# Emptying a filler tile one step earlier, and starting the next projection before the last attention values, in a hybrid decoder layer

## The chip, the cores and the metric

The kernel runs on one core of a Trainium2 chip. The metric is the device time of one execution in microseconds. The core has a matrix engine (TensorE, PE in the rows; PEld is its loading of weights), VectorE (DVE), ScalarE (ACT), GpSimd (POOL) and SyncE (SP); each takes its own instructions strictly in order and waits on semaphores for the others. DMA transfers are issued by SP and POOL here.

## What is computed

One layer for 512 new tokens and 8 running sequences of 8 tokens each (576 columns in all). What matters here is the attention branch and what is multiplied after it:

```python
h = rmsnorm(x, p['norm1_w'])
proj = h @ p['w_in']
q, k, v, z, xbc, dt, ga, gb = jnp.split(proj, _split_points(IN_SIZES), axis=-1)
...
attn = stick_breaking_attention(q, k_all, v_all, sb_bias, past)
...
merged = jax.nn.sigmoid(ga) * (attn @ p['w_pa']) + jax.nn.sigmoid(gb) * (y @ p['w_pb'])
x = x + merged @ p['w_out']
```

In stick-breaking attention a weight is the sigmoid of its logit times the product of (1 - sigmoid) over later keys, a running product along the keys. All products are taken in three parts (high x high, low x high, high x low) to hold float32 accuracy. After this come the SSD mixer, the output projection and the feed-forward part.

## The kernel before, in words

**A tile** is one 128 x 576 result of a dense product, kept in one of two buffers of PSUM, `G[0]` and `G[1]` (`tile_banks`), by the parity of its number. `product` (L437 to L453) multiplies one slice of 128 inputs into it with six matmuls; a tile has 8 slices (`KD`). It waits before the first slice until the buffer is free (`tile_free`), which the engine that reads the tile signals. A weight chunk of 128 columns is loaded by SP, copied to `w_hi` by ScalarE (`make_hi`, L417) and its rest to `w_lo` by VectorE (`make_lo`, L423); chunks alternate between two buffers.

**Attention** is a software pipeline of 60 steps (`STEPS_A`) over 57 units: one for new keys, 16 for cache pages, 40 for the prompt (8 pairs of heads, five units each). In step t TensorE makes the logits of unit t (L1120), ScalarE their sigmoid (L1679) and one minus it (L1692), VectorE the running product and the weights one step later (`weigh`, L2177 and L2179), TensorE turns the weights of unit t-2 (L1145), ScalarE copies them out (`read_weights`, L1715) and VectorE takes the rest (L2223). In the step three after a pair's last unit TensorE multiplies values with weights, 16 matmuls (`weigh_values`, L1200), whose result lies in `G[0]`; ScalarE (L1748) and VectorE (L2242) read it, and ScalarE (L1753) and VectorE (L2248) split it into the two parts that the projection will multiply.

**Fillers** are 22 tiles (both gates and six tiles of z) whose slices are laid between this work: `filler_steps` gives each step up to two slices in its middle (after the logits) and up to two (for the prompt one) at its end. They all use `G[1]`, since `G[0]` holds turned keys and the values' result; so filler f has tile number `T_FILL + 2 * f`. When a tile is finished one place is left empty, then the next tile begins. 17 of the 22 end in the middle of their step: 3 while pages are read, and 14 in the prompt's steps 17, 20, 23 and so on to 56; three end at the end of a page step, filler 21 at the end of step 57, and filler 0 before the steps.

`gate_tile(f)` on ScalarE waits until the tile is done, copies it out through the sigmoid (L1723), which frees the buffer, and then makes the `w_hi` of chunk f+2. It stands at the head of the step after the one in which the tile ended. VectorE makes that chunk's `w_lo` in that next step, and GpSimd stores the tile (`store_gate`, L806).

**The drain** is steps 57 to 59, without logits. Step 59 has the last values product. Behind it TensorE waits until VectorE has read `G[0]` (`pv_read`, 16) and makes the eight tiles of `attn @ w_pa` (L1233 to L1239); the first uses `G[0]`. The result of each is multiplied by VectorE (L2281) with a gate tile that GpSimd brings back from memory (`ga_in`, L811). Before GpSimd asks for it, it does in its order: store filler 21, make `a_seq` (L823), clear a scratch array with six DMAs (L826), wait for them, set a diagonal (L828).

Of the kernel before, what the change touches and what calls it, by code (L numbers as in the profile page):

```python
# [123 lines left out]
def build(nc, x_prompt, x_sample, cache_k, cache_v, page_table, state_ssm, state_conv, norm1_w, w_in,  # L124
# [21 lines left out]

    T_FILL = N_FIRST
    assert T_FILL % 2 == 1
    T_PA = T_FILL + 2 * N_FILL - 1
    T_SSD = T_PA + KD  # L150
    T_OUT = T_SSD + NG * (10 + KD) - len(Z_EARLY)
    T_FFN = T_OUT + KD
# [2 lines left out]
    with ExitStack() as ctx:  # L155
# [5 lines left out]
        def sem(name):  # L161
            if name not in sems:
                sems[name] = ctx.enter_context(nc.semaphore(name))
            return sems[name]
# [275 lines left out]
        def product(pe, t, w, x, start=True, stop=True, rows=P, step=0, i=0, onto=False):  # L440


            if start:
                pe.wait_ge(tile_free[t % 2], half(t, step, i) + 1)
            last = len(w) - 1
            for k, ((wh, wl), (xh, xl)) in enumerate(zip(w, x)):
                for h in range(2):
                    out = G[t % 2][0:rows, h, 0:HALF]
                    nc.tensor.matmul(out, wh, xh[:, HALVES[h]], start=start and k == 0, stop=False, skip_group_check=onto)  # L449
                    nc.tensor.matmul(out, wh, xl[:, HALVES[h]], start=False, stop=False, skip_group_check=onto)  # L450
                for h in range(2):
                    out = G[t % 2][0:rows, h, 0:HALF]
                    mm = nc.tensor.matmul(out, wl, xh[:, HALVES[h]], start=False, stop=stop and k == last, skip_group_check=onto)  # L453
            return mm
# [112 lines left out]
                    tile_end[f] = (n - 1) // 2  # L567
        late_tiles = [f for f in range(N_FILL) if f not in tile_end]
        ends_at = {t: [f for f in tile_end if tile_end[f] == t] for t in range(-1, STEPS_A)}

        def filler_tile(f):
            return T_FILL + 2 * f
# [50 lines left out]
        def out_hi(k):  # L623
            return qo[:, 2 * k, :]
# [364 lines left out]
        def _(pe):  # L989
# [50 lines left out]
            def fill(todo):  # L1040


                for f, k in todo:
                    c, t = C_FILL + f, filler_tile(f)
                    if k == 0:
                        pe.wait_ge(split, c + 1)
                    mm = product(pe, t, [(w_hi[:, c % 2, k, :], w_lo[:, c % 2, k, :])], [(x_hi[:, k, :], x_lo[:, k, :])], start=k == 0, stop=k == KD - 1)
                    if k == KD - 1:
                        mm.then_inc(tile_done, 2 if f else 1)
# [154 lines left out]
            def turn_outputs(part):  # L1204
# [5 lines left out]
                    mm = pe.transpose(out_bank(part)[:, b * P:(b + 1) * P], o_rows[:, b * P:(b + 1) * P], ident[:, :])  # L1210
                mm.then_inc(sem("o_turned"), 1)

            for t in range(STEPS_A):
                if t < NU:
                    logits(units[t])
                if is_page(t + 1):
                    turn_keys(t + 1)
                for part in range(2):
                    if t == 2 * SEQS * (part + 1) + 6:
                        turn_outputs(part)  # L1220
                fill(filler[1 + 2 * t])
                if t >= 3:
                    weigh_values(units[t - 3])
                if 2 <= t < NU + 2:
                    if t == 2 * SEQS + 6:
                        pe.wait_ge(sem("o_lo_made"), 1)
                    turn_weights(units[t - 2])
                fill(filler[2 + 2 * t])
            fill(filler[-1])

            pe.wait_ge(sem("pv_read"), 2 * KD)
            pe.sem_inc(tile_free[0], N_FILL - 1)
            for n in range(KD):  # L1233
                c, t = C_PA + n, T_PA + n
                pe.wait_ge(split, c + 1)
                for k in range(KD):
                    if n == 0:
                        pe.wait_ge(sem("o_split"), k + 1)
                    mm = product(pe, t, [(w_hi[:, c % 2, k, :], w_lo[:, c % 2, k, :])], [(out_hi(k), out_lo(k))], start=k == 0, stop=k == KD - 1)  # L1239
                mm.then_inc(tile_done, 1)  # L1240


# [290 lines left out]
        def _(act):  # L1533
# [220 lines left out]

            for t in range(STEPS_A + 2):
                for f in ends_at.get(t - 1, []):
                    gate_tile(f)
                if t < NU:
                    stick(units[t])
                if is_page(t + 1):  # L1760
                    read_keys(t + 1)
                if t < NU:
                    stick_rest(units[t])
                for part in range(2):
                    if t == 2 * SEQS * (part + 1) + 6:
                        outputs_hi(part)
                if 2 <= t < NU + 2:
                    read_weights(units[t - 2])
                for part in range(2):
                    if t == 2 * SEQS * (part + 1) + 3:  # L1770
                        copy_outputs(part)
                if 4 <= t < NU + 4 and units[t - 4]["kind"] == "prompt" and units[t - 4]["last"]:
                    pair_hi(units[t - 4]["p"])
                if 3 <= t < NU + 3 and units[t - 3]["kind"] == "prompt" and units[t - 3]["last"]:
                    lower_half(units[t - 3]["p"])
# [853 lines left out]
```

## Time and profile before

| | us |
|---|---|
| median of 3 runs | 1492.87 |
| lowest, highest | 1485.05, 1494.22 |
| the profiled execution's own time | 1489.72 |
| its span, first to last instruction | 1488.2 |
| TensorE matmul busy | 1417.5 (95%) |
| VectorE busy | 822.6 (55%) |
| ScalarE busy | 654.4 (44%) |
| GpSimd busy | 222.4 (15%) |
| TensorE idle before the first matmul of a slice of `x_hi`, whole span | 18.0, of it 14.0 released by ScalarE's L1723 |

The chain of waits of the page is empty here (its last piece is a DMA that was issued at the end), so the profile is read by waits and by timelines. The steps of attention run from about 140 to 428 us, the `attn @ w_pa` tiles follow until 484 us; the SSD mixer, the output projection and the feed-forward products come behind them.

### The profile page before, as it was taken

Reading aid. Unit: us, or ns where it says so; the run is one execution under the profiler, and the core shown is the slowest. Engines: PE = TensorE matmul, PEld = TensorE weight load, DVE = VectorE, ACT = ScalarE, POOL = GpSimd, SP = SyncE. Lnnn points to the kernel's source line nnn. Section 1 sums busy time; section 2 is a strip of 40 time slices with the busy share of each in tenths; the row PEclk is TensorE's granted clock in tenths of the full one; section 3 lists DMA queues with packets and bytes.
Section 4 is the critical chain, followed back from the end, with each engine's and each line's share of the span. In section 5 each row is a group of like instructions: output and inputs, shape, how many; then the busy total and the mean of one; then the engine's idle time right before and its main releaser. Section 6 shows DMA issues by size and latency. Waiting matters only on the chain. (4 is left out here: it accounts for less than half of the span.)

```text
span 1488.2 us, 27180 instructions
## 1 busy us (share of the span) xinstructions
PE 1417.5 (95%) x10645; PEld 1332.1 (90%) x10645; DVE 822.6 (55%) x1194; ACT 654.4 (44%) x1086; POOL 222.4 (15%) x398
## 2 busy tenths in 40 slices
PE   4999999989989999999999999999999999999997
PEld 4998777888879988889988988899999999999997
DVE  3554545887742566777687675774444444442221
ACT  4565454766631354574364473434432333331221
POOL 3002232000021213322222213211100000000000
PEclk9999999999999999999999999999999999999999
DMA  3225674221256433434334425352223222223331
GB/s 116 72 78 169 177 213 146 67 61 59 67 126 195 97 92 109 113 103 114 101 114 109 114 72 177 109 191 71 86 71 88 81 85 85 85 81 100 95 93 48
DMA packets 201109, 157.35 MB, mean 106 GB/s; under 512 B 13672, under 2 KB 187216, under 8 KB 200959
## 3 DMA queue, kind: packets, MB, share of 16 engines
q1 hardware_dynamic: 175394, 97.93, 23.0%
q0 software_dynamic: 25232, 57.70, 13.5%
q8 instruction: 66, 1.08, 0.3%
q10 hardware_dynamic: 384, 0.37, 0.1%
q14 instruction: 33, 0.27, 0.1%
HBM read 132.04 MB, written 23.91 MB: 105 GB/s over the span
## 5 line engine op out<-in xcount | busy, mean ns | idle before, releaser
L449 PE MATMUL tile_banks<-x_hi,w_hi 128*128 128x288 f32 (+1 forms) x1808 | 530.9, 308 | 18.0 <-ACT gate_out L1723 14.0
L450 PE MATMUL tile_banks<-x_lo,w_hi 128*128 128x288 f32 (+1 forms) x1808 | 508.3, 296 | 0.0
L453 PE MATMUL tile_banks<-x_hi,w_lo 128*128 128x288 f32 (+1 forms) x1808 | 386.9, 295 | 0.0
L449 PEld LDWEIGHTS tile_banks<-x_hi,w_hi 128*128 128x128 f32 (+1 forms) x1808 | 341.9, 189 | 33.5 <-issue 25.3
L450 PEld LDWEIGHTS tile_banks<-x_lo,w_hi 128*128 128x128 f32 (+1 forms) x1808 | 342.1, 189 | 4.7 <-issue 3.6
L423 DVE TENSOR_TENSOR w_lo<-w_raw,w_hi 128x1024 fp32r<-128x1024 f32 (+2 forms) x169 | 208.3, 1233 | 174.7 <-ACT w_hi L417 173.5
L453 PEld LDWEIGHTS tile_banks<-x_hi,w_lo 128*128 128x128 f32 (+1 forms) x1808 | 291.4, 188 | 0.4
L417 ACT ACTIVATE w_hi<-w_raw 128x1024 fp32r<-128x1024 f32 (+2 forms) x169 | 175.7, 1039 | 103.6 <-PE tile_banks L453 102.0
L450 PE MATMUL tile_banks<-f_lo,w_hi 128*128 128x288 f32 x352 | 98.3, 295 | 0.0
L449 PE MATMUL tile_banks<-f_hi,w_hi 128*128 128x288 f32 x352 | 97.8, 294 | 0.0
L453 PE MATMUL tile_banks<-f_hi,w_lo 128*128 128x288 f32 x352 | 73.9, 291 | 0.0
L980 POOL DMA_DIRECT2D out_y_prompt<-y_tok x8 | 6.2, 779 | 410.1 <-ACT y_tok L2050 410.1
L2037 ACT ACTIVATE f_hi<-prod 128x576 f32 (+1 forms) x22 | 15.1, 686 | 118.3 <-DVE prod L2575 118.3
L450 PEld LDWEIGHTS tile_banks<-f_lo,w_hi 128*128 128x128 f32 x352 | 66.2, 188 | 0.0
L449 PEld LDWEIGHTS tile_banks<-f_hi,w_hi 128*128 128x128 f32 x352 | 66.0, 188 | 0.0
L2306 DVE SCALAR_TENSOR_TENSOR conv_acc<-conv_src,conv_par,conv_acc 128x600 f32<-128x600 f32 x72 | 60.8, 844 | 2.5
L1837 ACT ACTIVATE conv_src<-tile_banks 128x288 f32<-128x288 f32 x24 | 9.9, 412 | 118.6 <-PE tile_banks L453 118.6
L787 POOL DMA_DIRECT2D v_page<-in_cache_v x64 | 34.5, 539 | 160.0 <-issue 160.0
L449 PE MATMUL tile_banks<-y_hi,w_hi 128*128 128x288 f32 x192 | 56.8, 311 | 0.2 <-DVE w_lo L423 0.2
L453 PEld LDWEIGHTS tile_banks<-f_hi,w_lo 128*128 128x128 f32 x352 | 56.5, 188 | 0.0
L450 PE MATMUL tile_banks<-y_lo,w_hi 128*128 128x288 f32 x192 | 53.7, 295 | 0.0
L2177 DVE TENSOR_TENSOR_SCAN after_w<-rest,zero_col 128x128 f32<-128x128 f32 (+2 forms) x64 | 52.4, 818 | 0.3
(378 smaller groups left out, 2501.2 us busy)
## 6 DMA issues: line engine op xcount, KB each, us to landing
w_raw<-in_w_in SPq DMA_DIRECT2D x68, 512.0 KB, 3.8
w_raw<-in_w_gate SPq DMA_DIRECT2D x22, 512.0 KB, 3.8
w_raw<-in_w_up SPq DMA_DIRECT2D x22, 512.0 KB, 3.7
k_page<-in_cache_k SPq DMA_DIRECT2D x64, 128.0 KB, 2.6
v_page<-in_cache_v POOLq DMA_DIRECT2D x64, 128.0 KB, 3.0
old<-in_state_ssm POOLq DMA_DIRECT2D x32, 256.0 KB, 3.4
out_ssm_sample<-old POOLq DMA_DIRECT2D x32, 256.0 KB, 2.8
w_raw<-in_w_pb SPq DMA_DIRECT2D x16, 512.0 KB, 3.6
```

Of the source, the lines that this page charges most:

```text
L417: nc.scalar.activation(w_hi[:, c % 2, 0:tiles, 0:width], w_raw[:, c % 2, 0:tiles, 0:width], ACT.Copy).then_inc(hi_made, 1)
L423: nc.vector.tensor_tensor(w_lo[:, c % 2, 0:tiles, 0:width], w_raw[:, c % 2, 0:tiles, 0:width], f32(w_hi[:, c % 2, 0:tiles, 0:width]), ALU. ...
L449: nc.tensor.matmul(out, wh, xh[:, HALVES[h]], start=start and k == 0, stop=False, skip_group_check=onto)
L450: nc.tensor.matmul(out, wh, xl[:, HALVES[h]], start=False, stop=False, skip_group_check=onto)
L453: mm = nc.tensor.matmul(out, wl, xh[:, HALVES[h]], start=False, stop=stop and k == last, skip_group_check=onto)
L787: eng.dma_start(v_page[:, n % V_SLOTS, :], cache_v[0, bass.ds(page_of(eng, x, k), 1)].rearrange("o p h d -> p (o h d)")).then_inc(sem(f"v_ ...
L980: eng.dma_start(y_prompt[0].rearrange("(c p) n -> p c n", p=P)[:, :, bass.ds(P * i, P)], y_tok[:, 0:NC, :]).then_inc(sem("y_out"), 16)
L1837: eng.activation(dst[:, 3:3 + HALF], G[t % 2][:, 0, 0:HALF], ACT.Copy)
L2037: eng.activation(f_hi[:, bass.ds(2 * i + n, 1), :], prod2[:, n:n + 1, :], ACT.Copy).then_inc(sem("f_hi_made"), 1)
L2177: link(eng.tensor_tensor_scan(out=after_w[:, slot, edge - width:edge][:, ::-1], data0=rest[:, slot, cols][:, ::-1], data1=zero_col[:, 0:1] ...
L2306: ins = eng.scalar_tensor_tensor(out=dst, in0=src[:, w:w + m], scalar=conv_par[:, w * CT + ct:w * CT + ct + 1], in1=dst, op0=ALU.mult, op1 ...
```

## The change

ScalarE empties a tile that ended in the middle of its step in that same step: after its sigmoid work, before it copies out the turned weights. `ends_mid` lists these tiles; the 5 others stay as they were. VectorE's and GpSimd's orders are unchanged. `T_PA` grows by one, so that the first `w_pa` tile lies in `G[1]` and not in `G[0]`; all later tiles swap buffers with it. Its first four slices are issued at the end of step 58, the next three in step 59 ahead of the last values product, the eighth behind it. The wait for `pv_read` now stands behind that tile.

```diff
--- before.py
+++ after.py
@@ -146,7 +146,7 @@
 
     T_FILL = N_FIRST
     assert T_FILL % 2 == 1
-    T_PA = T_FILL + 2 * N_FILL - 1
+    T_PA = T_FILL + 2 * N_FILL
     T_SSD = T_PA + KD
     T_OUT = T_SSD + NG * (10 + KD) - len(Z_EARLY)
     T_FFN = T_OUT + KD
@@ -567,6 +567,8 @@
                     tile_end[f] = (n - 1) // 2
         late_tiles = [f for f in range(N_FILL) if f not in tile_end]
         ends_at = {t: [f for f in tile_end if tile_end[f] == t] for t in range(-1, STEPS_A)}
+        ends_mid = {t: [f for f, k in filler[1 + 2 * t] if k == KD - 1] for t in range(STEPS_A)}
+        assert not late_tiles and not filler[2 * STEPS_A - 2] and not filler[2 * STEPS_A - 1]
 
         def filler_tile(f):
             return T_FILL + 2 * f
@@ -1210,6 +1212,15 @@
                     mm = pe.transpose(out_bank(part)[:, b * P:(b + 1) * P], o_rows[:, b * P:(b + 1) * P], ident[:, :])
                 mm.then_inc(sem("o_turned"), 1)
 
+            def first_pa(slices):
+
+                c = C_PA
+                pe.wait_ge(split, c + 1)
+                for k in slices:
+                    pe.wait_ge(sem("o_split"), k + 1)
+                    mm = product(pe, T_PA, [(w_hi[:, c % 2, k, :], w_lo[:, c % 2, k, :])], [(out_hi(k), out_lo(k))], start=k == 0, stop=k == KD - 1)
+                return mm
+
             for t in range(STEPS_A):
                 if t < NU:
                     logits(units[t])
@@ -1219,6 +1230,8 @@
                     if t == 2 * SEQS * (part + 1) + 6:
                         turn_outputs(part)
                 fill(filler[1 + 2 * t])
+                if t == STEPS_A - 1:
+                    first_pa(range(PG, KD - 1))
                 if t >= 3:
                     weigh_values(units[t - 3])
                 if 2 <= t < NU + 2:
@@ -1226,17 +1239,16 @@
                         pe.wait_ge(sem("o_lo_made"), 1)
                     turn_weights(units[t - 2])
                 fill(filler[2 + 2 * t])
-            fill(filler[-1])
+                if t == STEPS_A - 2:
+                    first_pa(range(PG))
+            first_pa(range(KD - 1, KD)).then_inc(tile_done, 2)
 
             pe.wait_ge(sem("pv_read"), 2 * KD)
-            pe.sem_inc(tile_free[0], N_FILL - 1)
-            for n in range(KD):
+            pe.sem_inc(tile_free[0], N_FILL)
+            for n in range(1, KD):
                 c, t = C_PA + n, T_PA + n
                 pe.wait_ge(split, c + 1)
-                for k in range(KD):
-                    if n == 0:
-                        pe.wait_ge(sem("o_split"), k + 1)
-                    mm = product(pe, t, [(w_hi[:, c % 2, k, :], w_lo[:, c % 2, k, :])], [(out_hi(k), out_lo(k))], start=k == 0, stop=k == KD - 1)
+                mm = product(pe, t, [(w_hi[:, c % 2, k, :], w_lo[:, c % 2, k, :]) for k in range(KD)], [(out_hi(k), out_lo(k)) for k in range(KD)])
                 mm.then_inc(tile_done, 1)
 
 
@@ -1754,7 +1766,8 @@
 
             for t in range(STEPS_A + 2):
                 for f in ends_at.get(t - 1, []):
-                    gate_tile(f)
+                    if f not in ends_mid.get(t - 1, []):
+                        gate_tile(f)
                 if t < NU:
                     stick(units[t])
                 if is_page(t + 1):
@@ -1764,6 +1777,8 @@
                 for part in range(2):
                     if t == 2 * SEQS * (part + 1) + 6:
                         outputs_hi(part)
+                for f in ends_mid.get(t, []):
+                    gate_tile(f)
                 if 2 <= t < NU + 2:
                     read_weights(units[t - 2])
                 for part in range(2):
```

The place is ScalarE's order in step 29, in which filler 11 ends and a values product lies as well. `wt_hi` is the copy of turned weights, `o_part` the reading of the values' result, `gate_out` the tile and `w_hi` the chunk behind it. Before:

```order
L1679 ACTIVATE beta<-spare_bank,bias_all 128x256 x2
L1692 ACTIVATE rest<-beta 128x512
L1715 ACTIVATE wt_hi<-spare_bank 128x4x128
L1748 ACTIVATE o_part<-tile_banks 64x512 x2
L1723 ACTIVATE gate_out<-tile_banks 128x576
L417 ACTIVATE w_hi<-w_raw 128x1024
```

With the change:

```order
L1691 ACTIVATE beta<-spare_bank,bias_all 128x256 x2
L1704 ACTIVATE rest<-beta 128x512
L1735 ACTIVATE gate_out<-tile_banks 128x576
L417 ACTIVATE w_hi<-w_raw 128x1024
L1727 ACTIVATE wt_hi<-spare_bank 128x4x128
L1760 ACTIVATE o_part<-tile_banks 64x512 x2
```

The tile and the chunk's `w_hi` have moved ahead of `wt_hi` and `o_part`; the four other rows kept their order.

The second place is TensorE's order in the drain, at the last turning of weights (`<-ident,beta`) in step 58. Before, the last values product (`wt_hi,v_hl`) follows it directly:

```order
L453 MATMUL tile_banks<-x_hi,w_lo 128x288 x2
L1145 MATMUL spare_bank<-ident,beta 128x128 x4
L1200 MATMUL tile_banks<-wt_hi,v_hl 128x512
L1200 MATMUL tile_banks<-wt_lo,v_hl 128x512
L1200 MATMUL tile_banks<-wt_hi,v_hl 128x384
```

With the change products of the projection (`qo`) follow it:

```order
L453 MATMUL tile_banks<-x_hi,w_lo 128x288 x2
L1147 MATMUL spare_bank<-ident,beta 128x128 x4
L449 MATMUL tile_banks<-qo,w_hi 128x288
L450 MATMUL tile_banks<-qo,w_hi 128x288
L449 MATMUL tile_banks<-qo,w_hi 128x288
```

Seven slices stand there, 35 such rows, and then the values product begins:

```order
L450 MATMUL tile_banks<-qo,w_hi 128x288
L453 MATMUL tile_banks<-qo,w_lo 128x288 x2
L1202 MATMUL tile_banks<-wt_hi,v_hl 128x512
L1202 MATMUL tile_banks<-wt_lo,v_hl 128x512
L1202 MATMUL tile_banks<-wt_hi,v_hl 128x384
```

The eighth slice comes behind that product:

```order
L1202 MATMUL tile_banks<-wt_hi,v_hl 128x128
L1202 MATMUL tile_banks<-wt_lo,v_hl 128x128
L449 MATMUL tile_banks<-qo,w_hi 128x288
L450 MATMUL tile_banks<-qo,w_hi 128x288
L449 MATMUL tile_banks<-qo,w_hi 128x288
```

The values product has thus moved behind seven of the eight slices of the first tile.

## Rows read from the trace of the kernel before

**Rows 1.** Waits of TensorE, 125 to 490 us: us in total, times, longest.

```profile
PE tile_banks L449 <- ACT gate_out L1723: 14.0, 14, 2.0
```

**Rows 2.** Timeline of TensorE: start, us, operation; in brackets idle before it and releaser.

```profile
303.42 0.37 PE L449 MATMUL tile_banks<-x_hi,w_hi 128*128 128x288 f32 x1 [1.97 <-ACT gate_out L1723]
...
313.82 0.37 PE L449 MATMUL tile_banks<-x_hi,w_hi 128*128 128x288 f32 x1 [0.60 <-ACT gate_out L1723]
...
327.59 0.37 PE L449 MATMUL tile_banks<-x_hi,w_hi 128*128 128x288 f32 x1 [1.29 <-ACT gate_out L1723]
...
338.21 0.37 PE L449 MATMUL tile_banks<-x_hi,w_hi 128*128 128x288 f32 x1 [0.66 <-ACT gate_out L1723]
...
351.27 0.37 PE L449 MATMUL tile_banks<-x_hi,w_hi 128*128 128x288 f32 x1 [0.78 <-ACT gate_out L1723]
...
415.39 0.37 PE L449 MATMUL tile_banks<-x_hi,w_hi 128*128 128x288 f32 x1 [1.32 <-ACT gate_out L1723]
```

**Rows 3.** Timeline of ScalarE in step 29.

```profile
300.77 0.60 ACT L1715 ACTIVATE wt_hi<-spare_bank 128x512 fp32r<-128x512 f32 x1 [3.11 <-PE spare_bank L1145]
301.39 1.21 ACT L1748 ACTIVATE o_part<-tile_banks 64x512 f32<-64x512 f32 x2
302.62 0.65 ACT L1723 ACTIVATE gate_out<-tile_banks 128x576 f32<-128x576 f32 x1
303.17 1.05 ACT L417 ACTIVATE w_hi<-w_raw 128x1024 fp32r<-128x1024 f32 x1
```

**Rows 4.** Windows: length, busy time of each engine, granted clock, DMA share.

```profile
300.00:375.00 75.00, 67.73 (x488) 63.03 (x488) 59.83 (x92) 50.49 (x87) 3.25 (x6) 0.98 0.22 66
```

**Rows 5.** Timeline of VectorE, steps 30 and 31, up to the end of unit 30's weights.

```profile
306.35 0.69 DVE L2223 TENSOR_TENSOR wt_lo<-spare_bank,wt_hi 128x512 fp32r<-128x512 f32 x1 [0.62 <-ACT wt_hi L1715]
...
310.60 0.29 DVE L2179 TENSOR_TENSOR beta<-beta,after_w 128x128 f32<-128x128 f32 x1
```

**Rows 6.** Timeline of TensorE, step 32, turning of unit 30's weights.

```profile
311.90 0.60 PE L1145 MATMUL spare_bank<-ident,beta 128*128 128x128 f32 x4
```

**Rows 7.** Timeline of ScalarE in step 38.

```profile
336.93 0.60 ACT L1715 ACTIVATE wt_hi<-spare_bank 128x512 fp32r<-128x512 f32 x1 [0.59 <-PE spare_bank L1145]
```

**Rows 8.** Timeline of VectorE in step 38.

```profile
337.56 0.69 DVE L2223 TENSOR_TENSOR wt_lo<-spare_bank,wt_hi 128x512 fp32r<-128x512 f32 x1 [0.87 <-ACT wt_hi L1715]
```

**Rows 9.** Timeline of TensorE, values product of step 39.

```profile
339.85 0.39 PE L1200 MATMUL tile_banks<-wt_hi,v_hl 128*128 128x512 f32 x1
```

**Rows 10.** Windows of 2 us in which the clock fell during attention.

```profile
366.00:368.00 2.00, 2.00 (x11) 2.00 (x12) 1.90 (x5) 1.97 (x4) 0.54 (x1) 0.67 0.38 147
368.00:370.00 2.00, 2.00 (x11) 1.99 (x11) 0.27 (x1) 0.67 (x3) 0.00 (x0) 0.50 0.00 0
```

**Rows 11.** Timeline of TensorE in the drain and the first projection tiles.

```profile
425.31 0.50 PE L1200 MATMUL tile_banks<-wt_hi,v_hl 128*128 128x512 f32 x1 [2.46 <-DVE wt_lo L2223]
...
430.50 0.37 PE L449 MATMUL tile_banks<-qo,w_hi 128*128 128x288 f32 x1 [2.43 <-PEq L1232]
...
438.47 0.29 PE L449 MATMUL tile_banks<-qo,w_hi 128*128 128x288 f32 x1
...
445.19 0.40 PE L449 MATMUL tile_banks<-qo,w_hi 128*128 128x288 f32 x1 [0.31 <-DVE w_lo L423]
```

**Rows 12.** Timeline of ScalarE in the drain, filler 21.

```profile
422.45 0.65 ACT L1723 ACTIVATE gate_out<-tile_banks 128x576 f32<-128x576 f32 x1 [2.62 <-PE tile_banks L453]
```

**Rows 13.** Timeline of VectorE in the drain.

```profile
430.90 0.69 DVE L2248 TENSOR_TENSOR qo<-o_sum,qo 128x512 fp32r<-128x512 f32 x1 [0.70 <-ACT qo L1753]
...
443.24 0.76 DVE L2281 TENSOR_TENSOR gate_out<-tile_banks,ga_in 128x576 f32<-128x576 f32 x1 [11.65 <-DMA ga_in<-gates_dram]
```

**Rows 14.** Timeline of GpSimd in the drain.

```profile
439.55 0.56 POOL L828 DMA_DIRECT2D sums_dram<-ones  x1 [9.52 <-DMA sums_dram<-zeros]
```

**Rows 15.** Windows of 2 us after two pauses of TensorE.

```profile
432.00:434.00 2.00, 2.00 (x10) 2.00 (x10) 0.00 (x0) 0.00 (x0) 0.00 (x0) 0.50 1.49 223
...
488.00:490.00 2.00, 2.00 (x8) 1.78 (x8) 0.00 (x0) 0.66 (x4) 0.81 (x2) 0.50 0.46 62
```

## The prediction, made before the changed kernel was run

> **What bounds the kernel now.** I first read the waits of TensorE over attention and the tiles behind it [rows 1]: 14.0 us in 14 waits are one kind, the first slice of a filler tile held back until ScalarE has emptied the tile before it. The timeline [rows 2] shows these waits one by one. There are 14 because 14 fillers end in the middle of a prompt step; they come in six sizes: 0.60 (3 times), 0.66 (3), 0.78 (3), 1.29 (2), 1.97 (2) and 1.32 (once), together 13.96. The reader should see that each stands on TensorE itself, which has no other work in order at that point. Then the windows [rows 4]: in 75 us of attention TensorE is busy 67.7, VectorE 59.8, ScalarE 50.5. TensorE sets the pace, but VectorE is 80% busy, so a delay given to VectorE may come back. Last I read the drain [rows 11 to 14], engine by engine.
>
> **Part one: the tile is emptied in its own step.** ScalarE does the same work; the 0.65 for the tile and 1.05 for the next chunk's `w_hi` [rows 3] only change places with the copy of the turned weights. In step 29 the order was: wait 3.11 for the turned weights behind the values product, 0.60, then `o_part` 1.21, then the tile. Now tile and `w_hi` fit into those 3.11 and TensorE's wait of 1.97 goes. In a step without a values product, as step 38 [rows 7], ScalarE was idle 0.59 from 336.34 to 336.93, waiting for the turning that TensorE does behind the tile. The tile can be emptied from about 336.5 to 337.15, and TensorE wants the buffer at 338.21 - 0.66 = 337.55 [rows 2]: this wait goes too.
>
> What the move costs: `wt_hi` comes later, and VectorE's `wt_lo` behind it. In step 38: tile to 337.15, `w_hi` to 338.1, `wt_hi` to 338.6 and not 337.53, so `wt_lo` starts at 338.65 and not 337.56 [rows 8] and ends at 339.33. TensorE's values product needs it, and would now start at 339.85 - 0.66 = 339.19 [rows 9]. So 0.15 of the 0.66 is given back. If the 1.29 of step 35 has just been gained, VectorE is behind by about 0.3 more and 0.45 of 1.29 + 0.66 is given back: 1.5 is kept.
>
> The other place is behind the 1.97. VectorE finished the weights of unit 30 at 310.60 + 0.29 = 310.89 and TensorE turned them at 311.90 [rows 5, 6], a margin of 1.0. TensorE would be there 1.97 earlier, at 309.93; VectorE gains only the 0.62 that it had waited for `wt_hi` [rows 5], and ends at 310.3. TensorE waits 0.4 there. ScalarE's (1 - sigmoid) of a new unit needs the same weights to be finished, so it gets to filler 12 late and 0.2 more is left there: of 1.97 + 0.60 I keep 2.0. In the next values product VectorE waits anyway, so nothing is carried on from pair to pair.
>
> The 0.78 waits I count as gone. For the 1.32 in front of filler 21 no logits lie between, so TensorE wants the buffer right after the turning: 0.6 is left. The sum: 2 x 2.0 (1.97 with 0.60) + 2 x 1.5 (1.29 with 0.66) + 3 x 0.78 + 0.60 + 0.5 (the 0.60 and the 0.66 that stand alone) + 0.7 (the 1.32) = 11.1 us. Its bounds: 14.0 if VectorE is never late, and about 1 if the 1.1 us by which `wt_hi` moved in step 38 returned at the 12 tiles that end without a values product (14.0 - 13.2). I take 11.1, near the top, because the rows show a margin at most of these places. The three fillers that end mid-step under the pages had no wait before; their ScalarE move is hidden by its waits for turned weights. I count nothing.
>
> With the 1.97 goes something else. Behind the second of the two, at 365.96, the granted clock was 0.67 and then 0.50 for 2 us each [rows 10]: 1.2 GHz and not 2.4. Work lost: 0.66 + 1.00 = 1.66 us. Behind the first of them it did not fall. I take it that without the pause the clock stays up: 1.6 us. Bounds 0 and 1.6.
>
> **Part two: seven slices before the last values product.** Before, TensorE had two pauses [rows 11]: 2.46 until 425.31 and 2.43 until 430.50. Tile 1 begins at 438.47 and ends at 445.19 - 0.31 = 444.88, 6.41 for 8 slices, 0.80 each. With the change, in times of before: ScalarE frees filler 21's buffer at 422.45 + 0.65 = 423.10 [rows 12], TensorE starts at 423.25, and seven slices last to 428.85. The values product (425.31 to 430.50 - 2.43 = 428.07, 2.76) runs to 431.6. The eighth slice needs the last pair's low part; VectorE ended it at 430.90 + 0.69 = 431.59, 3.52 behind the values product [rows 13], so now at 435.1. That is a new pause of 3.5 in place of 4.9 in two. Tile 0 ends at 435.9, 2.6 earlier than 438.47, and tile 1 at 442.3.
>
> But tile 2 needs a `w_lo` which stands on VectorE behind the multiplication of tile 0 with its gate, and this started at 443.24 only because the gate's transfer landed then; VectorE had waited 11.65 for it [rows 13]. The transfer hangs on GpSimd, which waited 9.52 for its clearing DMAs until 439.55 [rows 14]; these follow the store of filler 21, not TensorE's projection. Their time moves with filler 21, by part one, and not by part two. So tile 2 starts at 445.19 less part one's gain, as before. **Part two is worth no more than 0.3**, the 0.31 that tile 2 waited for its `w_lo`; the 2.6 turn into a pause of 2.9 in front of tile 2. Bounds: 2.6 if the transfer came sooner, -1.7 by the clock (below). Changing the buffers' parity adds no instruction and I count it at nothing: the buffer of every later tile is read by the same engine in the same order.
>
> **The sum** on the profiled execution's own 1489.7: 1489.7 - 11.1 - 1.6 - 0.3 = 1476.7. That execution was 3.2 below the median of the three runs (1492.9), whose spread is 9; the forecast for a median is thus about 3 higher: **1480**.
>
> **The rivals.**
>
> *A. The clock falls once more in front of tile 2.* TensorE would pause 3.5 before slice eight and 2.9 before tile 2. Pauses of 2.43 and 2.20 were each followed by a clock of 0.50 [rows 15]. A fall behind the first pause is hidden, it shortens the second; one behind the second is not: 1.7 us as in attention [rows 10]. That gives 1481.7. Against it: if the first pause lowers the clock, tile 1 ends near 444 and the second pause is only about 1.3. The Trainium skill (TensorE: Matmul & The Clock Gate, section on HAM oscillation) says that waits between bursts of matmuls send the clock back to half rate so that the next burst starts slow; it speaks against part two, and by it the sum would be about 1.7 higher. Chance 0.2.
>
> *B. VectorE takes the gain back.* The moved `wt_hi` makes `wt_lo` and the next weights late at most tiles, or ScalarE reaches the tile late, so that the change does not empty it earlier. For it: VectorE is 80% busy [rows 4], and margins of 0.2 to 1.0 us are what I worked with. Against it: it waits in every values product. Between 1 and 7 us remain in all: 1486 to 1492 for a median, middle 1489. Chance 0.17.
>
> *C. Everything goes.* No wait is left (14.0), the clock stays up (1.6), and the transfer comes early enough for 2.6 in the drain: 18.2, 1474.7 for a median. Chance 0.14.
>
> *D. Slower: VectorE becomes the bound.* If VectorE had no slack, each of the 17 mid-step tiles would push `wt_hi` and all behind it by 0.65 + 1.05 = 1.7: 28.9 lost, 14.0 recovered, 1508. It decides once the pushes exceed VectorE's idle time. In 75 us that is 15.2 [rows 4], against 5 tiles with 8.5. So it should not: chance 0.04.
>
> **The numbers.** The forecast has 0.45, A 0.2, B 0.17, C 0.14, D 0.04. The range that leaves out the far parts of B, C and D is 1472 to 1489: it holds part one between 8 and 14, the clock either way, about 3 us between one median and the next, and the nearer half of B. One per cent is 14.9 us, about what a measurement of this kernel can tell from no change. C and the upper half of the forecast's spread lie beyond it: faster 0.30, same 0.66, slower 0.04.
>
> **What would show it.** In the waits of TensorE the line on ScalarE's tile copy falls from 14.0 to between 0.5 and 2, and new waits of some tenths on VectorE's weights (L1145 before) and `wt_lo` appear, 1 to 3 us in all. VectorE's wait for the gate's transfer stays near 8 us (its own last work, at 435.1, is 3.5 later than before, and the transfer lands at the same distance behind filler 21), and TensorE shows a pause of about 3.5 behind the last values product and one of 2 to 3 on `w_lo` in front of tile 2. From there on the two traces run at a constant distance of 11 to 13 us. I am wrong if filler 21 ends less than 8 us earlier than before, if tile 2 starts at another distance behind filler 21 than 22.7, or if the distance changes in the later stages.

## The result and the profile after

The changed kernel takes 1482.8 us (median of 9 runs, 1480.2 to 1485.1) against 1494.0 of the kernel before (9 runs, 1485.1 to 1496.2): a ratio of 0.9931 with a 95% interval of 0.9915 to 0.9948. That is 10.3 us by the ratio and 11.2 between the two medians, within the 1% at which the forecast called it the same, and inside its range of 1472 to 1489. The profiled execution took 1482.8 us with a span of 1481.3; the one of before, 1489.7 and 1488.2, lay 4.3 below that kernel's median.

The waits of TensorE in the changed kernel, 125 to 490 us (total, times, longest). The first row is a pause that the kernel before did not have; the third answers [rows 1]:

```profile
PE tile_banks L449 <- DVE qo L2263: 3.7, 1, 3.7
...
PE tile_banks L1202 <- DVE wt_lo L2238: 1.4, 3, 0.8
...
PE tile_banks L449 <- ACT gate_out L1735: 0.8, 2, 0.4
...
PE spare_bank L1147 <- DVE beta L2194: 0.8, 2, 0.4
...
PE tile_banks L449 <- DVE w_lo L423: 0.4, 1, 0.4
```

The waits on ScalarE's tile copy fell from 14.0 us to 0.8, and one of the two that are left (0.40) is the new one in front of the projection's first slice. Added to them are 0.8 on VectorE's weights (L2194) and 1.4 on `wt_lo`: 3.0 in all, so 11.0 of 13.96 are gone. The prediction had 11.1. Three of the places, in the timeline of TensorE:

```profile
275.85 0.50 PE L1202 MATMUL tile_banks<-wt_hi,v_hl 128*128 128x512 f32 x1 [0.84 <-DVE wt_lo L2238]
...
308.39 0.65 PE L1147 MATMUL spare_bank<-ident,beta 128*128 128x128 f32 x4 [0.39 <-DVE beta L2194]
...
402.77 0.37 PE L449 MATMUL tile_banks<-x_hi,w_hi 128*128 128x288 f32 x1 [0.41 <-ACT gate_out L1735]
```

The first is the values product behind the 0.66 that stood alone; it gives back 0.84, where about 0.15 was worked out. The second is the turning of unit 30's weights [rows 6], which now waits 0.39 (0.4 was worked out). The third stands where 1.32 stood in front of filler 21 [rows 2], with 0.41 left (0.6 was worked out).

The drain, as TensorE, ScalarE, VectorE and GpSimd have it; these answer [rows 11 to 14]:

```profile
422.54 0.58 PE L449 MATMUL tile_banks<-qo,w_hi 128*128 128x288 f32 x1 [3.67 <-DVE qo L2263]
...
432.61 0.40 PE L449 MATMUL tile_banks<-qo,w_hi 128*128 128x288 f32 x1 [0.44 <-DVE w_lo L423]
```

```profile
409.78 0.65 ACT L1735 ACTIVATE gate_out<-tile_banks 128x576 f32<-128x576 f32 x1 [2.53 <-PE tile_banks L453]
```

```profile
421.70 0.69 DVE L2263 TENSOR_TENSOR qo<-o_sum,qo 128x512 fp32r<-128x512 f32 x1 [0.69 <-ACT qo L1765]
...
430.67 0.76 DVE L2296 TENSOR_TENSOR gate_out<-tile_banks,ga_in 128x576 f32<-128x576 f32 x1 [8.28 <-DMA ga_in<-gates_dram]
```

```profile
426.96 0.56 POOL L830 DMA_DIRECT2D sums_dram<-ones  x1 [9.59 <-DMA sums_dram<-zeros]
```

Filler 21 is emptied 12.67 us earlier than before (409.78 for 422.45), and tile 2 of the projection starts 12.58 earlier (432.61 for 445.19), so 22.83 behind filler 21 where it was 22.74. The early start of tile 0 brought nothing to that point: VectorE waited 8.28 for the gate's transfer, and GpSimd 9.59 for its clearing DMAs (9.52 before).

But the pause in front of tile 2 is 0.44 and not the 2.9 of the forecast. The windows of 2 us around slice eight show why (length, busy time and instructions of PE, PEld, DVE, ACT, POOL, then the granted clock, DMA share, GB/s):

```profile
418.00:420.00 2.00, 0.87 (x7) 0.72 (x5) 0.40 (x1) 1.07 (x2) 0.00 (x0) 1.00 1.38 259
420.00:422.00 2.00, 0.00 (x0) 0.00 (x0) 1.27 (x3) 0.74 (x2) 0.00 (x0) 0.68 1.34 185
422.00:424.00 2.00, 1.47 (x6) 1.50 (x7) 0.39 (x1) 0.00 (x0) 0.00 (x0) 0.50 1.33 162
424.00:426.00 2.00, 2.00 (x10) 2.00 (x9) 0.00 (x0) 1.06 (x1) 0.00 (x0) 0.50 0.68 88
426.00:428.00 2.00, 2.00 (x11) 2.00 (x11) 0.00 (x0) 0.00 (x0) 1.04 (x2) 0.61 0.02 3
428.00:430.00 2.00, 2.00 (x17) 2.00 (x16) 0.00 (x0) 0.00 (x0) 0.68 (x2) 1.00 0.68 201
```

The clock falls inside the pause of 3.67 and stays at 0.50, which is 1.2 GHz, until past 427: fully busy, TensorE starts 10 matmuls in the window at 424 and 17 in the one at 428. Tile 1 ends 22.4 behind filler 21, and 19.9 had been worked out at full clock. How much of it is lost differs from execution to execution: in a second profile of the same kernel the half clock lasted half as long, tile 1 ended 21.7 behind filler 21, and the pause in front of tile 2 was longer:

```profile
432.72 0.40 PE L449 MATMUL tile_banks<-qo,w_hi 128*128 128x288 f32 x1 [1.42 <-DVE w_lo L423]
```

### The profile page after: what moved, and what is told of

It reads as the page before. It is cut to its first block and busy times, and to the rows that moved or that the text cites. A ratio compares the mean times of both kernels' runs of the same rounds, so it can differ in the third digit from the quotient of the medians.

```text
span 1481.3 us, 27182 instructions
## 1 busy us (share of the span) xinstructions
PE 1422.3 (96%) x10645; PEld 1336.3 (90%) x10645; DVE 823.6 (56%) x1194; ACT 653.2 (44%) x1086; POOL 221.4 (15%) x398
```

## The stages side by side

The starts of VectorE's `w_lo` instructions cut the execution into stages. "Attention" is from filler 2's `w_lo` to filler 21's copy on ScalarE, "projection" from there to the `w_lo` of the first SSD chunk, "SSD" from it to the last SSD chunk's, "middle" to the 16th gate/up chunk's, "dense" to the last chunk's. All are differences of starts in the timelines, in us. "Falls" counts periods at half clock between 500 and 990 us, taken from windows of 10 us (one period takes 1.7 off the sum of clock times length).

| kernel (one profile each) | attention | projection | SSD | falls | middle | dense | span |
|---|---|---|---|---|---|---|---|
| before | 278.65 | 55.81 | 511.07 | 2 | 160.81 | 317.75 | 1488.2 |
| before again | 278.69 | 55.98 | 507.14 | 0 | 160.61 | 321.77 | 1490.9 |
| changed | 266.12 | 55.91 | 512.76 | 3 | 160.37 | 322.15 | 1481.3 |
| changed again | 266.30 | 56.22 | 508.64 | 0 | 161.20 | 322.88 | 1478.9 |
| part one alone | 265.99 | 56.66 | 508.43 | 1 | 163.18 | 321.85 | 1479.6 |
| part two alone | 280.47 | 55.75 | 511.17 | 2 | 161.87 | 322.88 | 1495.2 |
| eight slices behind | 266.56 | 55.68 | 512.31 | 3 | 162.89 | 318.65 | 1479.9 |
| 4 + 4, late transfer | 266.23 | 56.82 | 512.31 | 3 | 164.01 | 322.84 | 1487.2 |
| early transfer | 266.67 | 55.37 | 513.37 | 4 | 162.82 | 318.84 | 1482.0 |
| part one, early transfer | 266.32 | 56.84 | 511.19 | 2 | 162.67 | 318.64 | 1479.3 |
| `w_hi` later | 265.52 | 55.78 | 507.59 | 0 | 160.00 | 322.58 | 1473.4 |
| 4 + 4, early transfer | 266.70 | 50.49 | 511.38 | 3 | 160.82 | 322.89 | 1476.7 |
| the two together | 265.86 | 50.51 | 508.17 | 1 | 162.54 | 322.57 | 1473.3 |
| two tiles only | 274.45 | 56.66 | 509.65 | 2 | 160.61 | 321.26 | 1486.2 |

The columns "attention" and "projection" hold the effects of the edits. SSD, falls, middle and dense show no pattern that follows the edits, and the span adds everything up, which is why the whole times of single profiles mislead. The middle stage took 162.5 or more in the six profiles that have a period at half clock in it, and 160.0 to 161.9 in the others.

## Experiments

Every timed kernel ran beside the kernel before on the same chip.

**Part one alone.** The kernel before with `ends_mid` on ScalarE:

```diff
                 for f in ends_at.get(t - 1, []):
-                    gate_tile(f)
+                    if f not in ends_mid.get(t - 1, []):
+                        gate_tile(f)
...
+                for f in ends_mid.get(t, []):
+                    gate_tile(f)
                 if 2 <= t < NU + 2:
                     read_weights(units[t - 2])
```

Expected: 

> Only ScalarE's early emptying; the projection's first tile stays behind the values product and in G[0]. Theory 1 (part one is the whole gain): the waits on ScalarE's tile copy fall from 14.0 to about 1, filler 21 ends 12 to 13 us earlier than before (at about 410), tile 2 of the projection starts 22.7 behind filler 21's emptying, and the ratio to before is that of the full change, 0.993. Rival (part two carries 2 us or more of the gain): ratio 0.9945 or higher, and tile 2 starts 25 behind filler 21.

Measured: 1480.3 us, ratio 0.9906 (0.9882 to 0.9930). Attention is 265.99 long, as in the full change, and filler 21 is emptied at 409.11. The projection is 0.4 to 0.75 longer than in the two profiles of the changed kernel: tile 2 starts 23.71 behind filler 21, between the 22.7 of theory 1 and the 25 of the rival, and without a wait, since here TensorE itself is late (the clock fell behind both pauses of the drain). So part one is the gain.

**Part two alone.** The changed kernel with `gate_tile` back at the head of the next step:

```diff
                 for f in ends_at.get(t - 1, []):
-                    if f not in ends_mid.get(t - 1, []):
-                        gate_tile(f)
+                    gate_tile(f)
...
-                for f in ends_mid.get(t, []):
-                    gate_tile(f)
```

Expected: 

> Only the early start of the projection's first tile and its buffer; ScalarE empties every tile in the next step as before. Theory 1: the 14 waits stay at 14.0 us, tile 0 is done 2 to 3 us earlier, but tile 2 starts at the same distance behind filler 21 (22.7), so ratio 1.000. Rival (part two gains): 0.998 or lower. Second rival (the new pause lowers the clock): 1.001.

Measured: ratio 1.0004 (0.9986 to 1.0021), the projection 55.75: nothing, as expected. The 14 waits on ScalarE's tile copy in attention came to 14.0 us again; two more outside it make 16 and 14.8. Its attention is 1.8 longer than before's: TensorE waited 1.25 longer for key pages (3.21 against 1.96), and was busy 0.56 longer, with 6.83 us at half clock against 4.40. Here the clock falls behind both waits of 1.97, at 304 and at 368, and not behind the second alone [rows 10]:

```profile
304.00:306.00 2.00, 2.00 (x12) 1.98 (x10) 0.90 (x2) 0.79 (x2) 0.00 (x0) 0.50 0.34 126
...
368.00:370.00 2.00, 2.00 (x11) 1.98 (x10) 1.02 (x2) 1.07 (x4) 0.00 (x0) 0.50 0.38 147
```

**All eight slices behind the values product**, in the buffer and with the parities of the change:

```diff
-                if t == STEPS_A - 1:
-                    first_pa(range(PG, KD - 1))
...
-                if t == STEPS_A - 2:
-                    first_pa(range(PG))
-            first_pa(range(KD - 1, KD)).then_inc(tile_done, 2)
+            first_pa(range(KD)).then_inc(tile_done, 2)
```

Expected: 

> The full change, but all eight slices of the first tile stand behind the last values product; its buffer is still G[1] and all later tiles keep the swapped buffers. Theory 1: time as the full change and as part one alone, 0.993, since tile 2 waits for the gate's transfer in all of them. Rival (swapping the buffers' parity is what slows the gate and up products, seen as 0.81 us a slice after and 0.78 before): the feed-forward stretch is slower here and in the part-two kernel, and fast in the part-one kernel.

Measured: ratio 0.9943 (0.9922 to 0.9965), projection 55.68. Tile 2 starts 22.61 behind filler 21, once more on its `w_lo`:

```profile
432.66 0.40 PE L449 MATMUL tile_banks<-qo,w_hi 128*128 128x288 f32 x1 [2.74 <-DVE w_lo L423]
```

Tile 1 thus ends 19.88 behind filler 21, 2.5 sooner than in the changed kernel's first profile and in the kernel before. With the other buffer the first slice need not wait for `pv_read`, and that alone gives what part two was to give, without the pause of 3.67. The seven early slices are worth nothing. The rival on the buffers' parity fell: this kernel's dense stage is fast (318.65) and part one's, with the old parities, slow (321.85).

**The changed kernel again**, unaltered.

Expected: 

> The changed kernel unaltered, for one more profile. Theory: the slower pace of the feed-forward slices (0.81 and not 0.78) comes and goes from execution to execution; then the profiles of the four kernels of this call differ in it without regard to their buffers. Rival: it belongs to the swapped buffers and is here again.

Measured: ratio 0.9934 (0.9909 to 0.9959), dense stage 322.88, slow again. That alone would fit the rival; the kernel above decides against it, and so does the kernel before in its second profile (below).

**The gate's transfer earlier.** GpSimd asks for the first two gate tiles right behind the store of filler 21:

```diff
             for f in ends_at[STEPS_A - 1] + late_tiles:
                 store_gate(f)
+            for n in range(2):
+                gate_back(n)
...
-            for n in range(2):
-                gate_back(n)
```

Expected: 

> The full change, and GpSimd asks for the first two gate tiles right behind the store of filler 21, before it clears its scratch array. Theory 1 (the transfer's lateness ate part two): VectorE no longer waits for it, tile 2 starts when tile 1 ends, 20 us behind filler 21's emptying and not 22.8, and the time falls by 2.5 to 3 us against the full change: 0.991 of before. Rival (something else holds tile 2, as the chunk's w_hi or the clock behind the 3.7 us pause): tile 2 at 22 or more and 0.993.

Measured: ratio 0.9902 (0.9864 to 0.9939), and the projection 55.37, only 0.5 to 0.9 shorter than the changed kernel's two and not 2.5 to 3. VectorE no longer waits for the transfer, so half of theory 1 holds, but tile 2 comes hardly sooner, 22.42 behind filler 21 where the theory had 20 and the rival 22 or more. The ratio is near the theory's 0.991, but its interval holds the rival's 0.993 too. The rival's second guess is what holds tile 2: the clock, in windows of 4 us:

```profile
420.00:424.00 4.00, 0.44 (x5) 0.29 (x3) 2.06 (x3) 1.81 (x3) 0.00 (x0) 0.82 1.32 179
424.00:428.00 4.00, 3.90 (x16) 3.93 (x17) 1.69 (x2) 1.06 (x1) 0.00 (x0) 0.50 1.19 147
428.00:432.00 4.00, 4.00 (x28) 4.00 (x27) 0.29 (x1) 0.00 (x0) 1.57 (x3) 0.83 0.66 160
```

Tile 0's last slice and nearly half of tile 1 (3.7 of its 8.0 us) run at 1.2 GHz behind the pause of 3.66. Two limits of nearly the same length stood one behind the other, and taking one away shows the other.

**Part one alone with the earlier transfer** (the same edit on the part-one kernel).

Expected: 

> Part one alone with the same earlier transfer, the projection's first tile behind the values product. Theory 1: before, tile 2 waited only 0.3 beyond tile 1, so the earlier transfer brings 0.3 here, ratio 0.993; with the kernel above this makes part two worth 2.5 us once the transfer is early. Rival (part two worth nothing even then): both 0.991 or both 0.993.

Measured: ratio 0.9907 (0.9874 to 0.9940), projection 56.84 against 56.66: nothing. By the projection, part two with the early transfer is thus worth 56.84 - 55.37 = 1.5 us, not the 2.5 expected; the two ratios, 0.9902 and 0.9907, are as the rival had them, and their intervals are too wide to show 1.5 us. In both part-one kernels the clock fell twice in the drain, behind each of the two pauses of 2.4 to 2.5, and tile 1 ended later than in the kernel before, where it fell once.

**Slices four and four around the values product, transfer early:**

```diff
-                if t == STEPS_A - 1:
-                    first_pa(range(PG, KD - 1))
...
-            first_pa(range(KD - 1, KD)).then_inc(tile_done, 2)
+            first_pa(range(PG, KD)).then_inc(tile_done, 2)
```

Expected: 

> The full change with the earlier transfer, and the first tile's slices laid four before and four behind the last values product. Theory 1: the last pair's low part is ready 2.4 us earlier, three slices run while it is made, the pause of 3.7 falls to about 1.3, and with no long pause the clock need not fall: 2 to 4 us less than with the earlier transfer alone, 0.989 of before. Rival (the end of the gates' chain on VectorE is already the bound): no more than 0.991.

Measured: 1477.1 us, ratio 0.9884 (0.9848 to 0.9921), projection 50.49: 4.9 us shorter than with the earlier transfer alone and 5.4 shorter than the change. The pause fell to 1.18 and the clock stayed up:

```profile
418.00:422.00 4.00, 2.82 (x22) 2.59 (x21) 2.06 (x3) 1.34 (x3) 1.38 (x2) 1.00 1.34 226
422.00:426.00 4.00, 4.00 (x32) 4.00 (x32) 1.98 (x2) 1.06 (x1) 0.00 (x0) 1.00 1.25 163
426.00:430.00 4.00, 4.00 (x33) 4.00 (x32) 1.12 (x2) 1.06 (x1) 0.00 (x0) 1.00 0.87 173
```

VectorE in the same kernel; the third gate tile is the next to be late, 7.82 of waiting that TensorE does not yet feel:

```profile
422.16 0.76 DVE L2294 TENSOR_TENSOR gate_out<-tile_banks,ga_in 128x576 f32<-128x576 f32 x1 [1.15 <-PE tile_banks L453]
...
438.68 0.76 DVE L2294 TENSOR_TENSOR gate_out<-tile_banks,ga_in 128x576 f32<-128x576 f32 x1 [7.82 <-DMA ga_in<-gates_dram]
```

**Four and four, transfer late** (the same edit on the changed kernel).

Expected: 

> The full change with the slices laid four and four, but the gate's transfer as late as before. Theory 1 (transfer is the limit in the drain): the pause of 3.7 is gone and the clock stays up, tile 1 ends 18 to 19 behind filler 21's emptying, but tile 2 still starts at 22.7 and TensorE waits about 4 there; time as the full change, 0.993. Rival (the clock was the limit): tile 2 starts at 20 or less and 0.990.

Measured: ratio 0.9930 (0.9913 to 0.9948), projection 56.82, 6.3 longer than with the early transfer. The timeline of TensorE and its windows:

```profile
421.13 0.40 PE L449 MATMUL tile_banks<-qo,w_hi 128*128 128x288 f32 x1 [1.18 <-DVE qo L2261]
...
433.25 0.61 PE L449 MATMUL tile_banks<-qo,w_hi 128*128 128x288 f32 x1 [4.83 <-DVE w_lo L423]
```

```profile
431.00:433.00 2.00, 0.00 (x0) 0.00 (x0) 1.69 (x2) 0.00 (x0) 0.64 (x2) 0.98 0.09 37
433.00:435.00 2.00, 1.75 (x7) 1.75 (x8) 1.99 (x3) 0.00 (x0) 1.28 (x3) 0.50 0.62 196
435.00:437.00 2.00, 2.00 (x13) 2.00 (x12) 0.00 (x0) 0.00 (x0) 0.23 (x1) 0.67 0.81 232
```

Tile 2 starts at 433.25, 22.38 behind filler 21, as the theory had it, behind a pause of 4.83 in which TensorE had nothing to do. Tile 1 ended 17.55 behind filler 21 and the clock had stayed up until then. But at the end of this pause it falls, and tile 2 takes 7.80 where it took 6.45 in the changed kernel: that is rival A of the prediction, here in its pure form, at 1.35 and not 1.7. Neither edit gives anything alone (0.5 and -0.9); together they give 5.4.

**`w_hi` stays in the next step,** only the tile's copy moves:

```diff
                 for f in ends_at.get(t - 1, []):
                     if f not in ends_mid.get(t - 1, []):
                         gate_tile(f)
+                    else:
+                        make_hi(C_FILL + f + 2, after_tiles=filler_tile(f) + 1)
...
                 for f in ends_mid.get(t, []):
-                    gate_tile(f)
+                    gate_tile(f, hi=False)
```

Expected: 

> The full change, but of the two ScalarE instructions only the tile's emptying moves into its own step; the next chunk's w_hi stays at the head of the next step. Theory 1 (what is left of the gain is lost to the turned weights' copy, pushed by 1.7 us): the push is now 0.65, the waits on VectorE's weights and wt_lo (0.8 and 1.4 us) shrink to under 1 in all, and 1 us more is gained: 0.992. Rival (the loss is VectorE's own load, not the push): these waits stay at 2 us and 0.993.

Measured: ratio 0.9920 (0.9889 to 0.9951), attention 265.52, 0.6 to 0.8 shorter than in the changed kernel. The waits left:

```profile
PE spare_bank L1147 <- DVE beta L2197: 1.1, 3, 0.5
...
PE tile_banks L449 <- ACT gate_out L1735: 1.1, 3, 0.5
...
PE tile_banks L1202 <- DVE wt_lo L2241: 0.7, 1, 0.7
```

They come to 2.9, where the changed kernel's two profiles have 3.0 and 3.3. The waits on `wt_lo` halved, those on the weights rose. Some of the shorter stage is the wait for key pages, 2.3 us here against 2.4 and 3.3. The ratio is the 0.992 of theory 1, but the waits on the weights and `wt_lo`, which it put at under 1, come to 1.8. So theory 1 is not borne out: at most a few tenths hang on the push of `wt_hi`, and most of what is left does not.

**Both together** (`w_hi` later, four and four, transfer early).

Expected: 

> The transfer early, slices four and four around the last values product, and the chunk's w_hi left in the next step. Theory 1: the pieces add up: attention 0.5 to 0.8 us shorter, then 20 to 21 us from filler 21's emptying to the start of tile 2's successor as with the split alone; 1474 to 1477 by the level of the feed-forward pace, 0.987 to 0.989 of before.

Measured: 1476.7 us, ratio 0.9888 (0.9866 to 0.9910). Attention 265.86 and projection 50.51 add up. This version and the four-and-four split with the early transfer are the fastest here, and the intervals do not tell the two apart. That split, 0.9884 (0.9848 to 0.9921), lies below the changed kernel's 0.9931 (0.9915 to 0.9948), but the intervals just overlap; what shows its gain is the projection.

**Two tiles only.** Part one for fillers 11 and 16, those with waits of 1.97:

```diff
-        ends_mid = {t: [f for f, k in filler[1 + 2 * t] if k == KD - 1] for t in range(STEPS_A)}
+        ends_mid = {t: [f for f, k in filler[1 + 2 * t] if k == KD - 1 and t in (29, 44)] for t in range(STEPS_A)}
```

Expected: 

> Before, with the early emptying for two of the 17 tiles only, fillers 11 and 16, whose waits were 1.97 each. Theory 1: the waits on ScalarE's tile copy fall from 14.0 to about 10, the clock does not fall at 366 us nor at 303, and attention (from the w_lo at 143 us to filler 21's emptying) is shorter than before's 278.65 by 3.9 + 1.66 less the 0.4 that VectorE's weights cost twice: 273.5 to 274.5. Rival (the clock's falls there have nothing to do with the 1.97 waits): a fall is still seen and 275 or more.

Measured (one run, 1487.7 us): attention 274.45, inside the 273.5 to 274.5. The wait and its count:

```profile
PE tile_banks L449 <- ACT gate_out L1724: 10.5, 13, 1.3
```

No window of 2 us between 142 and 424 us has a lowered clock. The books of attention: 3.93 less waiting on the tiles (13.95 to 10.02; the 13th wait, 0.44, lies ahead of the stage), 0.77 more on VectorE's weights, 1.56 more on key pages (3.52 against 1.96), so TensorE was idle 1.60 less. It also spent 4.4 us fewer at half clock, 3.4 of them at 366 and 1.0 at the stage's start, which is worth 2.2. That makes 3.8, and the stage became 4.2 shorter. The remaining 0.4 I can't name, and the longer key-page waits and the 1.0 at the start were not foreseen, so the number falls into the expected interval partly by chance; the absence of the falls does not depend on it.

**The kernel before again.**

Expected: 

> The kernel before, unaltered, for one more profile. Theory: 14.0 us of waits again, the clock falls behind neither, one or both of the 1.97 waits, and its feed-forward slices run at 0.78 or at 0.81 us, the pace being no property of the kernel.

Measured (one run, 1492.4 us): 14.0 us in 14 waits, attention 278.69, the clock fell once behind such a wait, at 369, and the dense stage took 321.77 where the first profile of the same kernel took 317.75.

## Why the prediction held, point by point

**Waits on the tile's copy:** right in kind and in the total. 11.1 was forecast and 11.0 net was measured. Place by place the agreement is looser, and part of it is luck: unit 30's weights take back 0.39 (0.4 was worked out) twice, and the values product behind step 38's kind 0.27 (0.45) twice; the 0.2 that filler 12 was to keep did not appear, while the 0.66 that stands alone gave back 0.84 and not 0.15, and the 0.40 in front of the projection's first slice was in no sum.

**The clock in attention:** right in size. Attention became 12.53 us shorter: in it TensorE was idle 10.7 less (17.56 to 6.86) and busy 1.8 less at the same work. Its time at half clock went from 4.40 to 0.59 us, which is worth 1.9: 1.7 for the fall at 366, where 1.6 was forecast, and 0.2 at the stage's start. All fourteen profiles bear on the cause. Three have both waits of 1.97 (before, before again, part two alone), and the clock fell behind four of these six; in the two-tile kernel, which keeps all the shorter waits, it fell behind none, and between 148 and 410 us it fell in no profile with all of part one. It is shown that the falls go with these waits; what decides whether one comes is not.

**Part two worth 0.3:** right in size (-0.1 in the first profiles, -0.2 in the second), and the transfer was the bound. One step in it failed, "tile 1 at 442.3": it took the full clock. The fall behind the new pause of 3.67 made tile 1 end 2.5 later in one profile and 1.8 in the other, and the second pause of 2.9 shrank to 0.44 and 1.42. Rival A named this as what would weaken it, with a second pause of about 1.3. The Trainium skill (TensorE: Matmul & The Clock Gate, section on HAM oscillation) warns of waits between bursts; the trace agrees, with 0.50 behind 3.67 here and behind 4.83 in the late-transfer kernel. In the changed kernel the price is hidden behind the transfer, and that is why the early transfer alone earned 0.5. Nor were the early slices needed for an early tile 1: with all eight behind the values product it ended at the 19.9 of the forecast. That order with the early transfer was not run.

**The distance constant from there on:** wrong for the profiled pair. 12.6 us at tile 2 became 6.9 at the end, which the prediction had named as a sign of being wrong. The SSD stage has one fall more (512.76 against 511.07), two of its windows being

```profile
520.00:530.00 10.00, 7.89 (x52) 7.65 (x52) 6.89 (x10) 2.83 (x6) 0.07 (x1) 0.83 0.29 83
...
900.00:910.00 10.00, 9.77 (x60) 7.87 (x59) 6.20 (x15) 5.11 (x7) 2.31 (x3) 0.83 0.77 250
```

and the dense stage is 4.4 longer. I put none of that down to the change: the same two kernels, profiled again, have 508.64 against 507.14 and 322.88 against 321.77. In those two the spans differ by 12.0. The medians, over nine runs each, differ by 11.2.

**The sum:** 13.0 was forecast and 12.6 were there at tile 2; 10 to 11 arrive in the timed runs. Whether the difference is chance or costs of the swapped buffers stays open: the kernels with old parities have 0.9906 and 0.9907, those with the new ones and a late transfer 0.9930 to 0.9943 (0.9920 with `w_hi` later), the early transfer with new ones 0.9902, and the intervals overlap; the stages show no place for it.

## What to carry to other kernels

When an engine waits for a buffer, look for what stands ahead of the release in the releaser's own order: two instructions moved ahead of a copy that itself had to wait for the same matrix engine took 11 us out, and the margins of the third engine told the total of what would come back, though not each place. Work started early is worth only what the next late thing leaves, so follow each queue to the next meeting point before counting it; and where two limits end within a microsecond or two of each other, remove both in one kernel or both will look harmless.

## What the runs showed of the hardware

The windows of 100 us in the dense stage, of before and then of the changed kernel:

```profile
1200.00:1300.00 100.00, 100.00 (x764) 99.87 (x763) 43.51 (x48) 30.96 (x36) 0.00 (x0) 1.00 0.29 84
```

```profile
1200.00:1300.00 100.00, 100.00 (x746) 100.00 (x745) 43.10 (x48) 31.73 (x36) 0.00 (x0) 1.00 0.27 79
```

Both are fully busy at a granted clock of 1.00, yet one does 764 matmuls and the other 746. There are two paces of the same code, 6.30 and 6.44 us a tile (mean over 24) in these two, worth 4 us in the dense stage; 4 of 14 profiles have the fast one throughout (317.75 to 318.84); the changed kernel's first profile kept step with before's up to about 1137 us and then took the slower pace. Neither the kernel nor the buffers' parity decides which comes. I did not find its cause.

The SSD stage took 507 to 509 us with no or one period at half clock and 511 to 513 with two to four (one profile with two took 509.7). Such a period need not have a pause ahead of it: of the changed kernel's three, the one at 523 came with a pause of 2.1, but those at 769 and 905 began when TensorE had been busy without a break for 3 us or more. Between profiles the SSD stage differs by up to 6 us and the dense one by up to 5, so an edit worth less is to be read from the stage that it touches.

How often a pause of TensorE in attention, the drain or the projection was followed by a fall, counted where the half clock began within the pause or at most 1.3 us behind it: 3.67 us, five of five; 4.83, once of one; 2.43, five of five; 2.46, three of six; 1.97, four of six; 2.74, not in the one case; 1.18, in neither of two. Its length alone does not decide it.
